# Two products of 512 columns behind each of the second tile's level products, in the recurrent stage's first slots

## The reference

```python
amat = eye(C) + where(strict, einsum('bhncd,bhnsd->bhncs', kb, kc) * gamma, 0.0)
u = triangular_solve(amat, vc * beta[..., None])        # unit lower triangular
w = triangular_solve(amat, kb * exp(decay)[..., None])
aqk = where(tri, einsum('bhncd,bhnsd->bhncs', qc, kc) * gamma, 0.0)

def step(S, xs):                                        # one chunk after the other
    v_new = u_i - w_i @ S
    o = qd_i @ S + aqk_i @ v_new
    S = S * cd_i[..., None, None] + kd_i.T @ v_new
    return S, o
o = rms_norm(o, g_out) * silu(z)
y = concatenate([o_attn, o]) @ w_out
return h + y
```

## Time and profile before

| | us |
|---|---|
| median of 3 runs | 881.98 |
| lowest, highest | 881.82, 882.07 |
| the profiled execution | 885.48 |
| its span, first to last instruction | 883.7 |
| TensorE busy in it | 820.0 (93%) |
| VectorE busy | 618.0 (70%) |
| ScalarE busy | 381.9 (43%) |
| GpSimd busy | 250.8 (28%) |
| mean granted clock of TensorE | 0.97 |

### The profile page before, as it was taken

The page is one execution under the profiler, slowest core; times in us unless marked ns, Lnnn a source line. Parts: engine busy times, 40 slices in busy tenths (PEclk is TensorE's granted clock), DMA queues, the critical chain, the costliest instruction groups (busy, mean ns, idle before and its releaser), DMA issues.

```text
span 883.7 us, 16526 instructions
## 1 busy us (share of the span) xinstructions
PE 820.0 (93%) x6357; PEld 491.2 (56%) x6357; DVE 618.0 (70%) x1424; ACT 381.9 (43%) x1219; POOL 250.8 (28%) x254
## 2 busy tenths in 40 slices
PE   5999899999989999999799999995899889889897
PEld 2554434444446666666456666674676465556554
DVE  2344799999999999999456676675666575575532
ACT  3443757776882555554535555461222022022010
POOL 8000100000001464668435722104333233233200
PEclk9999999999999999999969999998599999999999
DMA  6252200030003020000201000106302022022011
GB/s 172 66 204 95 73 24 25 24 121 37 23 26 106 0 96 1 1 1 0 72 25 45 30 25 27 50 13 241 132 1 95 4 97 97 18 80 73 27 47 48
DMA packets 29298, 51.71 MB, mean 59 GB/s; under 512 B 3604, under 2 KB 11140, under 8 KB 29220
## 3 DMA queue, kind: packets, MB, share of 16 engines
q1 hardware_dynamic: 28676, 50.55, 17.0%
q0 software_dynamic: 544, 0.10, 0.3%
HBM read 40.11 MB, written 12.10 MB: 59 GB/s over the span
## 4 chain that ended last, share of the span: by engine, by line
PE 79%; DVE 11%; ACT 5%; issue 3%; DMA 1%; SPq 1%; POOL 0%; DVEq 0%; ACTq 0%
PE ps L1621 19%; PE ps L1599 11%; PE ps L1827 11%; PE ps L1476 6%; PE ps L1672 4%; PE ps L1661 4%; PE ps L1643 4%; DVE areaQ L1270 2%; PE ps L1573 2%; PE ps L1731 2%; PE ps L1527 1%; DVE areaQ L1400 1%; DMA areaC<-in_x 1%; PE ps L1707 1%; PE ps L1806 1%
## 5 line engine op out<-in xcount | busy, mean ns | idle before, releaser
L1137 DVE TENSOR_SCALAR_CACHE_REDUCE junk<-scores,iw 128x272 bf16<-128x272 f32 (+6 forms) x224 | 213.6, 954 | 8.2
L1621 PE MATMUL ps<-areaH,areaW 128*128 128x384 f32 (+1 forms) x576 | 168.1, 455 | 1.6 <-ACT areaQ L874 1.6
L1621 PEld LDWEIGHTS ps<-areaH,areaW 128*128 128x128 f32 x576 | 109.4, 190 | 59.9 <-issue 1.8
L1827 PE MATMUL ps<-areaW,areaQ 128*128 128x512 f32 x256 | 120.7, 606 | 8.0 <-DVE areaQ L1396 8.0
L692 POOL TENSOR_TENSOR staging<-staging,areaC 128x520 f32<-128x520 f32 x60 | 88.3, 1510 | 63.2 <-ACT areaC L912 63.2
L726 POOL TENSOR_TENSOR scores<-scores,masks 128x512 f32<-128x512 f32 x51 | 63.0, 1244 | 136.3 <-PE ps L1751 116.1
L1827 PEld LDWEIGHTS ps<-areaW,areaQ 128*128 128x128 f32 x256 | 45.1, 189 | 50.5 <-issue 40.2
L709 POOL TENSOR_TENSOR areaW<-scores,tmp 128x256 f32<-128x256 f32 (+1 forms) x64 | 43.5, 703 | 79.6 <-DVE small L1223 69.5
L1476 PE MATMUL ps<-areaW,areaH 128*128 128x460 f32 (+1 forms) x144 | 58.7, 561 | 2.0 <-DVE areaH L1059 1.9
L912 ACT ACTIVATE areaC<-areaC,small 128x520 f32<-128x520 f32 x60 | 42.5, 724 | 32.7 <-POOL staging L692 32.7
L1599 PE MATMUL ps<-areaH,areaW 128*128 128x512 f32 x128 | 56.3, 594 | 0.0
(11 more groups left out here) (276 smaller groups left out, 1349.1 us busy)
## 6 DMA issues: line engine op xcount, KB each, us to landing
areaW<-in_w_in SPq DMA_DIRECT2D x5, 2048.0 KB, 7.9
areaH<-row_factor_scratch SPq DMA_DIRECT2D x18, 256.0 KB, 5.1
areaC<-in_x SPq DMA_DIRECT2D x8, 512.0 KB, 3.6
areaW<-in_w_out SPq DMA_DIRECT2D x2, 2048.0 KB, 11.1
areaQ<-in_x SPq DMA_DIRECT2D x8, 512.0 KB, 5.9
y<-areaQ SPq DMA_DIRECT2D x8, 512.0 KB, 2.6
gate_a_scratch<-staging SPq DMA_DIRECT2D x8, 256.0 KB, 2.3
gate_g_scratch<-staging SPq DMA_DIRECT2D x8, 256.0 KB, 2.0
```

The source lines that it names most:

```text
L1137: tlink(V.tensor_scalar(junk[:, 0:n], scores[:, SC0[i]:SC0[i] + n], at, init, op, ALU.add, accum_out=cnt[:, i - 1:i]))
L1621: ins = mm(ps[:, n % 4, 0:hi - lo], wslot[:, g % 2, k, 128 * m:128 * m + 128], hT[:, k, lo:hi], start=k == 0, stop=k == KD - 1)
L1827: ins = mm(ps[:, 6 + half_, :], y, wslot[:, half_, k, :], start=k == 0, stop=k == 7)
```

## The change

Two things are added to TensorE's list, none is taken away. Ahead of `REST_ENTRIES` TensorE waits until the last tile of attention is gated (`s_on` at 8). And as it walks the first 33 entries, those ahead of the second tile's `p0`, it puts two products behind every x and y of the second tile: the identity, 128x128, by the first 512 columns of the convolved queries, into bank 6. Nobody reads that result, and the first product of the projection overwrites it. These are x and y of six levels, so 12 times two products. What the kernel returns is the same.

```diff
--- before.py
+++ after.py
@@ -1854,7 +1854,18 @@
                         scale_rows(k)
                 if step >= NP:
                     recurrent(RUN_OUT[step - NP][1])
-            recurrent(REST_ENTRIES)
+            def keep_at_work():
+
+                for _ in range(2):
+                    mm(ps[:, 6, :], ident, conv[:, 0, 3:3 + 512], start=True, stop=True)
+
+            pe.wait_ge(s_on, NB)
+            at = REST_ENTRIES.index((1, "p0"))
+            for k, (t, stage) in enumerate(REST_ENTRIES[:at]):
+                recurrent([(t, stage)])
+                if t == 1 and stage[0] in "xy" and stage != "yt":
+                    keep_at_work()
+            recurrent(REST_ENTRIES[at:])
 
 
 _INS = ["x", "meta_tokens", "rel_bias_table", "norm_gain", "w_in", "cq_norm_gain", "ckv_norm_gain", "w_uq", "w_ukv",
```

## The result

The changed kernel took 887.81 us in the median of four runs (885.53 to 888.38), the kernel before 881.9 (881.15 to 882.07). The ratio is 1.0064, with a 95% interval of 1.0045 to 1.0082: slower by 5.9 us. I had forecast 885.4 with a range of 881.5 to 889.5. The traced execution of the changed kernel is the one of 885.53 us, its span 883.8.

What follows compares the result with a forecast made beforehand. TensorE was taken as the bound (93% busy), with code gaps and half clock in the recurrent stage. 21.8 us of products against 4.5 of gap, 9 to 10 of clock, 4 of waits: 881.98 plus 3.4 gives 885.4 us, range 881.5 to 889.5.

Steps and rivals of the forecast that it cites:

- The cost of a pair: Two added 512-column products on TensorE at full clock: 1.82 us, bounds 1.72 to 1.92; 21.8 us for twelve.
- The gaps for code: TensorE idle in the second tile's levels, awaiting its next 16 KB of code: 0.8, 1.1 and a new 1.0 us.
- The sentence that sums up the cover: Set 21.8 us of products against some 4.5 us of gap, 9 to 10 of clock and 4 of covered waits.
- The own work: TensorE's existing work between the last six pairs, up to the third tile's x4: 9.7 us at full clock.
- (d): Last piece of the sum, from 626.3 us: six pairs, 10.9 us, plus 9.7 us of existing work, ending at 646.9.
- The new wait: Wait for the last gated attention tile, ahead of the second tile's first level product: costs nothing, nearly 4 us spare.
- the covered 0.24 us: Wait for VectorE ahead of the value product behind the third tile's x4: covered, turning +3.6 us into +3.4.
- The shift in the stage: Net lengthening of the recurrent stage with the clock kept, carried to the end: +3.4 us; this case had chance 0.58.
- The runs' median is 3.5 us lower, 881.98, and a shift carries over: Last step: profiled execution 885.48 us becomes 888.9 with the change; taken from the median instead, the forecast is 885.4 us.
- 9 to 10 us of clock: Time won back in the second tile's levels by TensorE running at full instead of half clock: 9 to 10 us.
- The clock falls once nevertheless: Rival: one to two pairs run at half clock, 3.7 us each, after a lightly used stretch; 887 to 890, chance 0.12.
- The cover is complete: Rival: code arrives in time, no gaps remain in the second tile's levels, so no change: 881.3 us; chance 0.18.

Runs made afterwards that it cites:

- the repeated trace: The changed kernel, unaltered, timed and traced again: median 888.29 us, ratio 1.0070 to the kernel before; this traced execution took 888.92 us.
- the late loads: Kernel before, with loads of tile 1 (but its row factors), w_out and tile 2 issued only once the second tile's level 8 is merged: 875.88 us.
- the run without products: The changed kernel with its wait and split loop but no added products: 882.11 us, ratio 1.0003 to the kernel before; its traced execution took 884.37 us.

## Why the prediction was right, and where it was not

- *The cost of a pair.* I took 1.82 us from a range of 1.72 to 1.92; it is 1.91 nearly everywhere (607.62 to 609.53), so that the term of 21.8 us should have been about 22.8. The projection row at the long end was the nearer one. The estimate from the Trainium skill ("TensorE: Matmul & The Clock Gate", Back-to-back issue gap, the formula for an isolated product, with four passes), 1.73, is 0.18 us per pair too low here.
- *The gaps for code.* Two were right in place: 0.8 and 1.1 us forecast, 0.67 and 1.60 in the trace with the clock kept, 0 and 0.53 in the other, where the first pair was slow. The third, of 1.0 us behind x16, did not appear in either. Counted on from the second gap (126 records), that piece ends inside the pair behind x16 and not ahead of it, at about 627.1 in the repeated trace; its transfer had ended at 625.1, and at the first two gaps work resumed 1.3 us after such an end. The sentence that sums up the cover also has it wrong: three gaps of 2.9 us in all instead of 6.5 are 3.6 us covered, not 4.5. The reading of the gaps as code behind loads, argued only, is now shown for most of their length, by the late loads and by the places of the gaps.
- *The own work.* x4 of the third tile comes 39.8 us behind x2 in the repeated trace (607.23 to 647.07), 39.4 in the first; (d) had 39.5.
- *The new wait* costs nothing, as the run without products shows, and the covered 0.24 us is gone.
- *The shift in the stage*, +3.4 us, is close to what the traces show against the first trace of before (+3.2, and +3.6 with the clock kept). Part of this is luck: the pairs were put 1.0 us too low, and a gap of 1.0 us was added that never came.
- *The step that failed* is "The runs' median is 3.5 us lower, 881.98, and a shift carries over". The profiled execution of before had its clock at half for about 31 us in this stage, one near the median about 24. The term "9 to 10 us of clock" that the products win back was read off an execution that had lost more than usual; in a usual one it is about 3 us less. With it the forecast would have been 881.98 + 3.4 + 2.9 = 888.3. That the measured 887.81 still lies in the stated range is owed to the width of the range, not to this step. The 3.5 us between the traced time and the median were the warning: I took them as an offset, without asking in which stage they lie. The Trainium skill ("TensorE: Matmul & The Clock Gate", Part 1) says that the point at which the clock returns varies from run to run with the same kernel; I had held the three close times of before against it. The traces agree with it in kind, 632 and 643 us, but the page gives half a microsecond either way, and here it is 11 us.
- *The rivals.* "The clock falls once nevertheless" (887 to 890) gives the measured time and was seen in the first trace, at the first pair, as described. But the repeated trace shows the same stage length without it, so the fall is not why the time is 887.8: the 1.1 us that it costs come out of the gap behind it. "The cover is complete" is refuted by the gaps that remain; even without any gap the products cost 10 us (885.89 against 875.88).

## What to carry to other kernels

Where one stage's clock varies from run to run, a single profiled execution can't price what the clock is worth: compare its time and mean granted clock with those of the timed runs first, and if it isn't near their median, look for the stage that differs. Idle work that keeps the clock up is itself paid for: here 22.8 us of it won back some 16 us of gaps, clock and waits, and even five single products put inside waits brought no gain that could be measured. And before a gap is filled, ask what makes it: moving the loads off the stretch in which TensorE uses up its code fastest was worth 6.7 us, and the 24 products on top of it cost 10.

## What the runs showed of the hardware

- TensorE's clock stayed at half through 24 to 34 us in which it was busy most of the time with small products (18.59 of 20.1 us in the earlier trace rows), and came back within one pair of products of 512 columns (3.09 us for the first pair, about 2 for the next). Busy time alone doesn't tell whether the clock returns. With the same instructions it was back near 632 us in one execution and near 643 in another. Nor does it tell whether it falls: after 1.29 us busy from 107.2 to 110.6 it was lost in the earlier trace rows, and after the same 1.29 us in the same stretch it was kept in the run without products.
- TensorE's instructions come by DMA in pieces of 16 KB, and small products use them up in a few us (126 records from 613.70 to 616.88). Behind full DMA engines (370 to 390 GB/s) a piece held TensorE up for 3 to 4 us, with the loads moved away for 0.7 to 1.0. The hold-up stands at a fixed count of instructions: added ones move it earlier in the list, record for record.
- Executions of one kernel differ by 0.7% here (879.5 to 885.8 us for before), and the mean granted clock sorts them roughly: 0.977 for the shortest, 0.966 for the longest.
